# Second block: mixing and experts in one stage by token tiles, and the forget-factor projection in column groups

## The chip, the cores and the metric

The kernel runs on one core of one Trainium2 chip. The metric is the time of one execution on the device, in microseconds (us). A core has a matrix engine (TensorE, PE in the rows, with its weight loads as PEld), a vector engine (VectorE, DVE), an activation engine (ScalarE, ACT), GpSimd (POOL), a queue engine that issues DMAs (SyncE, SP), and 16 DMA engines that all queues share.

## What is computed

Two blocks act on 256 tokens of width 1024, all in float32. The first block has two layers with recurrent (mLSTM), attention and Fourier branches and a feed-forward part; it also carries 256 context tokens in its first layer. The second block mixes (HGRN2 and S5), projects, and then sends each token through 128 retrieved experts. The parts that the change touches, cut from the reference:

```python
# first block, each layer: u = h @ w_in, of which 16 columns are the input and forget gates
i_f, f_f, i_b, f_b = jnp.split(u[4] + gate_b, 4, axis=-1)
...
# second block
mixed = jnp.concatenate([o_hg, o_s5], axis=-1) @ w_out[l]
x = x + gt1 * mixed
h2 = _rmsnorm_2(x, norm_ffn_w[l]) * (1.0 + sc2) + sh2
# experts, h2 in blocks of 128 tokens
qh = (hb @ w_q).reshape(tb, PEER_HEADS, 2, PEER_HALF)          # 8 heads, 2 x 128
s1 = jnp.einsum('thd,nd->thn', qh[:, :, 0], keys1)             # 128 keys each
s2 = jnp.einsum('thd,nd->thn', qh[:, :, 1], keys2)
v1, i1 = lax.top_k(s1, PEER_TOPK)                              # 16 and 16
v2, i2 = lax.top_k(s2, PEER_TOPK)
best, pos = lax.top_k(cand, PEER_TOPK)                         # 16 of the 256 sums
eidx = jnp.take_along_axis(cidx, pos, axis=-1)
gates = jax.nn.softmax(best.astype(jnp.float32), axis=-1).astype(hb.dtype)
act = jax.nn.gelu(jnp.einsum('td,thkd->thk', hb, u_tab[eidx]), approximate=False)
return jnp.einsum('thk,thkd->td', gates * act, v_tab[eidx])
```

## The kernel before

The program is a row of stages. In each stage every engine has its own instruction list, written out by hand, and waits on semaphores; at a stage's end all engines meet (the branch at L303). Nothing reorders the lists: what an engine waits for holds everything behind it.

**First block.** The first stage of a layer projects: `ml_job` multiplies eight 128-row pieces of the normed tokens by 128 columns of weights from a ring of four slots of 1 MB (L794 for 512 tokens across, L803 for 256). After the second job `gate_products` (L819) projects the 16 gate columns. DVE has spread them over 128 columns with zeros between (L1180 memset, L1184 copy), so that TensorE leaves each group of four at rows 0, 32, 64 and 96; ACT reads it there (L1028).

**Second block, mixing stage** (function `mixer`, from L2616). At its end `features` makes the GLU product, DVE and POOL gate the two halves of `merged` (`hg_gated`, `gated`), and TensorE multiplies by `w_out`: `out_tile` (L2805) for eight tiles of 128 columns with all 256 tokens across, each in eight steps. DVE adds each tile to the stream (L2967), ACT squares it (L3039), TensorE sums the squares with a matrix of ones (`out_sum`, L2812), DVE makes mean and reciprocal (L2970, L2971), ACT the root (L3041), DVE scales eight pieces (L2974) and ACT shifts them (L3044). SP meanwhile fetches the query weights of heads 0 to 3 into the ring.

**Second block, expert stage** (function `peer`). SP loads the keys and the query weights of heads 4 to 7 (L3437, L3439). TensorE makes the query of a head for 256 tokens (`query`, L3362), turns the tokens (L3388), and multiplies the query by the keys (`score`, L3380). DVE searches: a unit is one head and one tile of 128 tokens, so there are 16 units, numbered by tile and then by head, of 16 experts each. `halves` takes the best 16 of each half, `numbers` the best 16 of the 256 sums and their indices, `weights` the softmax. Then POOL issues one indirect DMA for each expert slot (L3207): 128 rows of 8 KB, half of it `u_tab`, half `v_tab`. There are 256 such gathers and a ring of eight buffers for them: gather e + 8 waits until TensorE is through with expert e; at the start, gathers 4 to 7 wait for queries 0 to 3, whose weights lie in their buffers. For each expert DVE makes the dot product with the token (L3230), ACT the GELU, the weight and a diagonal matrix (L3319, L3321, L3325), and TensorE adds the diagonal matrix times the `v_tab` half into two banks (L3425). The other steps are placed between the experts by `body`: the search of the unit ahead on DVE, one step of a late head's query after each expert on TensorE, the copies on ACT. After the last expert DVE and ACT do the final norm and SP stores.

## Time and profile before

| | us |
|---|---|
| median of 3 runs | 3245.86 |
| lowest and highest | 3235.61, 3633.01 |
| the profiled execution | 3240.87 |
| its span (first to last instruction) | 3239.0 |
| first indirect gather issued at | 2571.30 |
| last expert's dot product starts at | 3224.01 |
| TensorE busy | 3042.3 (94%) |
| VectorE busy | 1634.6 (50%) |
| ScalarE busy | 806.0 (25%) |
| mean DMA rate | 181 GB/s |

Positions in time are us from the start of the span. The busy shares are means over stages with different limits. The profiled execution took 1.9 us more than its span.

### The profile page before, as it was taken

How to read it: one execution, taken by the hardware profiler on the slowest of the kernel's cores; microseconds unless marked ns; L12 is line 12 of the kernel's file. 1: busy time of each engine (PE TensorE's matmuls, PEld its weight loads, DVE VectorE, ACT ScalarE, POOL GpSimd, SP SyncE). 2: the span in 40 equal slices, each digit the busy share in tenths (PEclk: the TensorE clock that was granted, in tenths of full speed). 3: DMA queues.
4: the chain of work that ended last, by engine and by line, in shares of the span. 5: the costliest groups of instructions: out<-in, count | busy, mean ns of one | idle time of the engine just before them, and what ended most of it. 6: DMA issues, size and time to landing. Idle time of an engine off the chain costs nothing. (4 is left out here: it accounts for less than half of the span.)

```text
span 3239.0 us, 33299 instructions
## 1 busy us (share of the span) xinstructions
PE 3042.3 (94%) x12432; PEld 2117.4 (65%) x12432; DVE 1634.6 (50%) x3601; ACT 806.0 (25%) x1852; POOL 337.4 (10%) x368
## 2 busy tenths in 40 slices
PE   8999999999999999999999999999988899877776
PEld 3566566758888888476776788888877744322222
DVE  3233444367763766313234467452046477777774
ACT  2122244311002100011213420010023244444443
POOL 0000000010000000100000000000000054444442
PEclk9999999999999999999999999999988999999999
DMA  6222111154432544642322234586331599999997
GB/s 236 75 69 63 54 52 53 52 162 130 137 117 65 169 145 132 196 145 80 101 81 65 78 120 151 201 319 223 125 125 55 202 418 420 420 421 421 420 416 306
DMA packets 280767, 584.76 MB, mean 181 GB/s; under 512 B 11736, under 2 KB 231768, under 8 KB 244256
## 3 DMA queue, kind: packets, MB, share of 16 engines
q0 software_dynamic: 51504, 338.98, 26.6%
q1 hardware_dynamic: 229104, 243.66, 23.3%
q8 instruction: 100, 1.64, 0.2%
q14 instruction: 59, 0.48, 0.0%
HBM read 581.52 MB, written 1.08 MB: 180 GB/s over the span
## 5 line engine op out<-in xcount | busy, mean ns | idle before, releaser
L794 PE MATMUL banks<-normed,weight_ring 128*128 128x512 f32 (+1 forms) x1280 | 484.5, 533 | 12.7 <-PEq L307 12.3
L794 PEld LDWEIGHTS banks<-normed,weight_ring 128*128 128x128 f32 x1280 | 243.1, 191 | 232.3 <-issue 221.4
L803 PE MATMUL banks<-weight_ring,normed 128*128 128x256 f32 x1408 | 322.5, 385 | 0.0
L3425 PE MATMUL banks<-weight_ring,work 128*128 128x512 f32 x512 | 249.8, 615 | 59.3 <-ACT work L3325 58.2
L3425 PE MATMUL banks<-work 128*128 128x512 f32 x512 | 252.9, 617 | 54.0 <-ACT work L3325 49.7
L803 PEld LDWEIGHTS banks<-weight_ring,normed 128*128 128x128 f32 x1408 | 266.4, 192 | 54.6 <-issue 19.4
L416 DVE CUSTOM_DVE_ANT_0 work<-work 128x1024 f32<-128x1024 f32 x176 | 209.3, 1223 | 108.2 <-DMA work<-ada_turned 88.5
L2091 PE MATMUL banks<-normed,weight_ring 128*128 128x256 f32 x1088 | 240.3, 384 | 8.7 <-ACT normed L2253 3.8
L2091 PEld LDWEIGHTS banks<-normed,weight_ring 128*128 128x128 f32 x1088 | 209.6, 193 | 38.8 <-ACT normed L2253 4.2
L3425 PEld LDWEIGHTS banks<-weight_ring,work 128*128 128x128 f32 x512 | 89.1, 190 | 199.2 <-ACT work L3325 134.8
L3425 PEld LDWEIGHTS banks<-work 128*128 128x128 f32 x512 | 88.8, 190 | 197.3 <-ACT work L3325 129.6
L1628 PE MATMUL banks<-branches,weight_ring 128*128 128x256 f32 (+1 forms) x656 | 207.5, 478 | 3.4 <-PEq L307 3.4
L3230 DVE CUSTOM_DVE_ANT_0 work<-work,branches 128x1024 f32<-128x1024 f32 x128 | 156.9, 1226 | 97.2 <-DMA work<-experts,branches 96.8
L3230 DVE CUSTOM_DVE_ANT_0 weight_ring<-weight_ring,branches 128x1024 f32<-128x1024 f32 x128 | 156.7, 1225 | 88.8 <-DMA weight_ring<-experts,branches 87.7
L1628 PEld LDWEIGHTS banks<-branches,weight_ring 128*128 128x128 f32 x656 | 124.6, 190 | 84.6 <-issue 75.5
L1652 PE MATMUL banks<-work 128*128 128x256 f32 x744 | 165.6, 379 | 0.0
L3207 POOL DMA_INDIRECT work<-experts,branches x128 | 136.1, 1064 | 242.5 <-PE banks L3425 170.1
L3207 POOL DMA_INDIRECT weight_ring<-experts,branches x128 | 142.0, 1110 | 180.7 <-PE banks L3425 173.1
L2091 PE MATMUL banks<-branches,weight_ring 128*128 128x256 f32 x736 | 159.8, 379 | 0.0
L1652 PEld LDWEIGHTS banks<-work 128*128 128x128 f32 x744 | 141.4, 190 | 19.2
L2091 PEld LDWEIGHTS banks<-branches,weight_ring 128*128 128x128 f32 x736 | 139.8, 190 | 19.0
L3319 ACT ACTIVATE work<-work 128x1 f32<-128x1 f32 x256 | 51.9, 203 | 334.2 <-DVE work L3230 333.9
(495 smaller groups left out, 3930.8 us busy)
## 6 DMA issues: line engine op xcount, KB each, us to landing
weight_ring<-w_in SPq DMA_DIRECT2D x98, 1024.0 KB, 5.2
weight_ring<-w_ffn_in SPq DMA_DIRECT2D x44, 1024.0 KB, 5.2
work<-ada_turned POOLq DMA_DIRECT2D x80, 512.0 KB, 3.8
work<-ada_turned POOLq DMA_DIRECT2D x16, 1536.0 KB, 9.2
weight_ring<-w_ffn_out SPq DMA_DIRECT2D x20, 1024.0 KB, 5.1
weight_ring<-w_out SPq DMA_DIRECT2D x12, 1024.0 KB, 5.2
weight_ring<-w_br_ml SPq DMA_DIRECT2D x8, 1024.0 KB, 5.1
weight_ring<-w_br_da SPq DMA_DIRECT2D x8, 1024.0 KB, 5.2
```

Of the source, the lines that this page charges most:

```text
L416: last = dve.tensor_tensor_reduce(out=out, in0=slot[:, t, :], in1=self.rows[:, row, :], scale=1.0, scalar=0.0, op0=ALU.mult, op1=ALU.add, ...
L794: last = pe.matmul(proj_bank(tile)[:, since:T], w[:, kk, half * P:(half + 1) * P], c.h[:, kk, since:T], start=kk == 0, stop=kk == KT - 1)
L803: last = pe.matmul(proj_bank(tile)[:, x * CHUNK:(x + 1) * CHUNK], c.h[:, kk, j * P:(j + 1) * P], w[:, kk, :], start=kk == 0, stop=kk == KT ...
L1628: ins = pe.matmul(bank(i)[:, cols(p0, p1)], w[:, k - at, half * P:(half + 1) * P], source[:, k, cols(p0, p1)], start=k == 0, stop=k == tot ...
L1652: last = pe.matmul(out[:, half * NCTX:(half + 1) * NCTX], left(k), right(k), start=k == 0, stop=k == KT // 2 - 1)
L2091: ins = pe.matmul(bank(i)[:, 0:NLAT], w[:, k - at, half * P:(half + 1) * P], source[:, k, lat], start=k == 0, stop=k == total - 1)
L3207: pool.indirect_dma_start(out=fetched[e % R], out_offset=None, in_=a["experts"], in_offset=bass.IndirectOffsetOnAxis(ap=experts_u[:, e:e + ...
L3230: dve.tensor_tensor_reduce(out=urows[e % R], in0=urows[e % R], in1=tokens[:, t, :], scale=1.0, scalar=0.0, op0=ALU.mult, op1=ALU.add, accu ...
L3319: act.activation(gl[:, r:r + 1], dot[:, at:at + 1], ACT.Gelu).then_inc(c.act_done, 1)
L3425: last = pe.matmul(c.banks[2 * t + half][:], diag[:, r, :], vrows[r][:, half * 512:(half + 1) * 512], start=e == t * H * K, stop=e == (t + ...
```

## The change

**Second block.** The expert stage becomes part of the mixing stage; `projection_and_experts` gives each engine's list, which `mixer` calls at its end, so no meeting of the engines stands between. The work from the output projection to the scores goes by tiles of 128 tokens: tile 0 is projected, normed and shifted, and head 0's query and score and the first search are made for tile 0 alone. The output projection of token tile 1 stands on TensorE around and behind that; its additions, squares, norm and shifts stand between the experts of units 0 and 1, and its turned tokens in unit 2. Queries and scores of heads 0 to 4 are made for each token tile apart (`PEER_QUERIES`: head, first tile, end), those of heads 5 to 7 for both. The search of unit 1 is no longer started before the first dot product but wholly between the first eight. The loads of `peer_wq` go to eight places outside the ring and are issued earlier, all but head 7's, which waits for the last tile of the output projection. Gathers 4 to 7 wait for the output projection of token tile 1, whose weights are in their buffers. ACT copies the turned tokens instead of DVE.

**First block.** The eight gate products are made in four column groups of 32 columns, two in each, into the rows 0 to 31, 32 to 63, 64 to 95 and 96 to 127 of another bank, after the first job. ACT copies the bank, and one product with the constant `gate_rows` (zeros and ones, a new part of the constants) adds the four and spreads them as before.

```diff
-PEER_EARLY, PEER_LATE, PEER_ROWS_UNIT = (0, 1, 2, 3), (4, 5, 6, 7), 5
+PEER_QUERIES = (*((head, 0, 1) for head in range(5)), *((head, 0, 2) for head in range(5, PEER_H)), *((head, 1, 2) for head in range(5)))
+PEER_AHEAD, PEER_BOTH, PEER_ROWS_UNIT = 3, 5, 5
+PEER_LOADS = ((0,), (1,), (2,), (3, 5, 6, 4), (7,))
...
     wg = scratch[:, 0:KT * 16].rearrange("p (k x) -> p k x", k=KT)
-    wg_apart = scratch[:, KT * 16:KT * 16 + KT * P].rearrange("p (k x) -> p k x", k=KT)
+    wg_apart = scratch[:, KT * 16:KT * 16 + KT * 32].rearrange("p (k x) -> p k x", k=KT)
+    gate_parts = scratch[:, KT * 48:KT * 48 + T]
...
             def gate_products():
+
                 pe.wait_ge(c.gate_apart, 1)
+                for first in range(2):
+                    for strip in range(4):
+                        last = pe.matmul(c.banks[1][32 * strip:32 * strip + 32, :], wg_apart[:, 2 * strip + first, :],
+                                         c.h[:, 2 * strip + first, :], start=first == 0, stop=first == 1)
+                last.then_inc(c.gate_product, 1)
+
+            def gate_total():
+                pe.wait_ge(c.gate_parted, 1)
                 pe.wait_ge(c.constants_loaded, 16)
-                for kk in range(KT):
-                    last = pe.matmul(c.banks[0][:], wg_apart[:, kk, :], c.h[:, kk, :], start=kk == 0, stop=kk == KT - 1)
-                last.then_inc(c.gate_product, 1)
+                pe.matmul(c.banks[0][:], c.constant("gate_rows"), gate_parts, start=True, stop=True).then_inc(c.gate_product, 1)
...
             for number in range(ML_JOBS):
                 ml_job(0, number)
+                if number == 0:
+                    gate_products()
                 if number == 1:
-                    gate_products()
+                    gate_total()
...
                 act.wait_ge(c.gate_product, 1)
+                act.activation(gate_parts, c.banks[1][:], ACT.Copy).then_inc(c.gate_parted, 1)
+                act.wait_ge(c.gate_product, 2)
...
-                apart = wg_apart.rearrange("p k (j x) -> p k j x", j=4)[:, :, :, 0:H]
-                dve.tensor_copy(apart, wg.rearrange("p k (j x) -> p k j x", j=4)).then_inc(c.gate_apart, 1)
+                dve.tensor_copy(wg_apart[:, :, 0:16], wg).then_inc(c.gate_apart, 1)
...
+                if i == SLOTS + 10:
+                    sp.wait_ge(c.pe_out, INPUTS)
+                    sp.wait_ge(c.vec_out, STATES)
+                    rest.early_loads(sp)
                 sp.wait_ge(c.product, FREED[i - SLOTS])
                 sp.dma_start(c.ring[:, i % SLOTS, 0:source.shape[1], :], source).then_inc(c.loaded[i % SLOTS], 16)
-            fetch(c, sp, following, lambda s: sp.wait_ge(c.out_product, 2 * s + 2))
+            rest.sync(sp)
...
+        for e in range(2 * H * K):
+            if e % K == 0:
+                pool.wait_ge(c.ranked, e // K + 1)
+            if e >= R:
+                pool.wait_ge(c.expert_done, e - R + 1)
+            elif e >= R // 2:
+                pool.wait_ge(c.out_product, KT + 2 * (e - R // 2 + 1))
...
+                if u == 0 and at < K // 2:
+                    next(parts[0], None)
+                if u == 0 and at >= K // 2:
+                    added(1, at - K // 2)
+                if u == 1 and at == 4:
+                    inverted(1)
+                if u == 1 and 7 <= at < 7 + KT:
...
+        for tile in range(KT):
+            added(0, tile)
+        inverted(0)
+        for k in range(KT):
+            out_scale(0, k)
+        search = Search(dve, 0)
+        for _ in search.halves():
+            pass
+        assert search.n == IN_HALVES
+        for _ in chain(search.numbers(), search.weights(1)):
+            pass
+        dve.wait_ge(c.token_copied, 2)
+        for u, t in units:
+            body(u, t)
...
+        act.activation(c.work[:, 7184:7185], c.constant("ones")[:, 0:1], ACT.Sqrt)
+        for tile in range(KT):
+            out_square(0, tile)
+        out_root(0)
+        for k in range(KT):
+            out_shift(0, k)
+        copy_query(0)
+        copy_scores(0)
+        copy_tokens(0)
+        exponentials(act, 1)
+        copy_query(1)
+        copy_scores(1)
+        copy_query(2)
+        for u, _ in units:
+            body(u)
...
+        pe.wait_ge(c.merged, 4)
+        pe.wait_ge(c.hg_gated, 2)
+        for tile in range(KT):
+            out_tile(0, tile, 0, 4)
+        pe.wait_ge(c.gated, 4)
+        for tile in range(KT):
+            out_tile(0, tile, 4, 8)
+            if tile >= 2:
+                out_sum(0, tile - 2)
+        pe.wait_ge(c.out_added, 2)
+        out_tile(1, 0, 0, 4)
+        out_sum(0, 6)
+        out_tile(1, 0, 4, 5)
+        out_sum(0, 7)
+        out_tile(1, 0, 5, 8)
+        out_tile(1, 1, 0, 8)
+        query(0)
+        turn_tokens(0)
+        score(0)
+        for tile in range(2, KT):
+            out_tile(1, tile, 0, 8)
+        query(1)
+        query(2)
+        score(1)
+        pe.wait_ge(c.token_copied, 2)
...
+                if PEER_AHEAD + u < len(PEER_QUERIES):
+                    query_product(PEER_AHEAD + u, at // KT, at % KT)
+                if PEER_AHEAD <= PEER_AHEAD + u - 1 < len(PEER_QUERIES) and at == 5:
+                    score(PEER_AHEAD + u - 1)
+                if u == 0 and at == 3:
+                    score(2)
+                if u == 1 and at == 2:
+                    pe.wait_ge(c.score_copied, 3)
+                    for tile in range(KT):
+                        out_sum(1, tile)
+                if u == 2 and at == 4:
+                    turn_tokens(1)
+                if u == PEER_ROWS_UNIT and at % 2 == 0:
+                    turn_rows(at // 2)
...
+    def early_loads(sp):
+        sp.dma_start(keys, a["keys"]).then_inc(c.wq_loaded[0], 16)
+        load(sp, 0)
+        load(sp, 1)
+
+    def sync(sp):
+        sp.wait_ge(c.hg_out, 2)
+        for head in (2, 3, 5, 6):
+            load(sp, head)
+        sp.wait_ge(c.gated, 4)
+        load(sp, 4)
+        sp.wait_ge(c.out_product, 2 * KT)
+        load(sp, 7)
```

How it moves instructions, at three places. In the lists `weight_ring` is the ring, `normed`, `merged`, `stream` and `branches` are large on-chip buffers, and the numbers are the output's rows and columns.

TensorE at the start of a layer of the first block; before:

```order
L794 MATMUL banks<-normed,weight_ring 128x512 x16
L819 MATMUL banks<-normed,merged 128x512 x8
L794 MATMUL banks<-normed,weight_ring 128x512 x32
L803 MATMUL banks<-weight_ring,normed 128x256 x16
L829 MATMUL banks<-constants_sb,work 128x4 x16
```

and now:

```order
L810 MATMUL banks<-normed,weight_ring 128x512 x8
L836 MATMUL banks<-normed,merged 32x512 x8
L810 MATMUL banks<-normed,weight_ring 128x512 x8
L843 MATMUL banks<-merged,constants_sb 128x512
L810 MATMUL banks<-normed,weight_ring 128x512 x32
L819 MATMUL banks<-weight_ring,normed 128x256 x16
```

The eight gate products moved ahead by one job and write 32 rows each; one product of 128 rows stands where they stood.

TensorE from the output projection to the first expert; before (L303 is the meeting of the engines, L3425 the first expert):

```order
L2805 MATMUL banks<-merged,weight_ring 128x256 x8
L2812 MATMUL banks<-normed,constants_sb 128x256 x4
L303 UNCONDITIONAL_BRANCH
L3349 UNCONDITIONAL_BRANCH
L3362 MATMUL banks<-normed,weight_ring 128x256 x16
L3388 MATMUL banks<-constants_sb,normed 128x128 x8
L3380 MATMUL banks<-branches 128x128 x4
L3388 MATMUL banks<-constants_sb,normed 128x128 x8
L3362 MATMUL banks<-normed,weight_ring 128x256 x32
L3380 MATMUL banks<-branches 128x128 x4
L3362 MATMUL banks<-normed,weight_ring 128x256 x16
L3380 MATMUL banks<-branches 128x128 x8
```

and now (L3413 the output projection, L3420 the sums of squares, L3436 queries, L3461 turned tokens, L3453 scores, L3512 experts):

```order
L3413 MATMUL banks<-merged,weight_ring 128x128
L3420 MATMUL banks<-normed,constants_sb 128x128
L3413 MATMUL banks<-merged,weight_ring 128x128 x11
L3436 MATMUL banks<-normed,stream 128x128 x16
L3461 MATMUL banks<-constants_sb,normed 128x128 x8
L3453 MATMUL banks<-branches 128x128 x2
L3413 MATMUL banks<-merged,weight_ring 128x128 x48
L3436 MATMUL banks<-normed,merged 128x128 x16
L3436 MATMUL banks<-normed,work 128x128 x16
L3453 MATMUL banks<-branches 128x128 x2
L3512 MATMUL banks<-work 128x512 x2
```

The meeting is gone, everything is 128 tokens across, and 48 of the output projection's products stand behind the first score.

DVE at the first dot products (L3230 before, L3238 now, where ISA is the dot product); before:

```order
L3173 TENSOR_TENSOR branches<-work 128x16
L3268 COPY branches<-banks 128x512 x2
L3181 TENSOR_REDUCE work<-work 128x1
L3182 RECIPROCAL work<-work 128x1
L3183 TENSOR_TENSOR branches<-work 128x16
L3129 COPY work<-branches 128x256
L3109 MAX work<-work 128x8 x2
L3115 MAX_INDEX work<-work 128x8 x2
L3120 MATCH_REPLACE work<-work 128x128 x2
```

and now, from the same place:

```order
L3175 TENSOR_TENSOR branches<-work 128x16
L3183 TENSOR_REDUCE work<-work 128x1
L3184 RECIPROCAL work<-work 128x1
L3185 TENSOR_TENSOR branches<-work 128x16
L3131 COPY work<-branches 128x256
L3111 MAX work<-work 128x8 x2
L3117 MAX_INDEX work<-work 128x8 x2
L3238 ISA work<-work,branches 128x1024
L3238 ISA work 128x1
L3122 MATCH_REPLACE work<-work 128x128 x2
L3111 MAX work<-work 128x8 x2
L3238 ISA work<-work,branches 128x1024
```

The first dot product stands after two steps of the second search, where before it stood after nearly the whole of its two parts.

## Rows read from the trace of the kernel before

**Rows 1.** Page, the span in 40 slices: busy DMA engines in tenths, and their rate.

```profile
DMA  6222111154432544642322234586331599999997
GB/s 236 75 69 63 54 52 53 52 162 130 137 117 65 169 145 132 196 145 80 101 81 65 78 120 151 201 319 223 125 125 55 202 418 420 420 421 421 420 416 306
```

**Rows 2.** Busy time by stretch: from:to, length, engines (x instructions), granted clock, DMA share, GB/s.

```profile
0.00:2359.00 2359.00, 2305.29 (x9464) 1732.28 (x9464) 1071.20 (x2249) 460.41 (x914) 55.44 (x107) 0.99 0.38 125
...
2538.90:2548.40 9.50, 1.77 (x9) 1.13 (x7) 5.91 (x11) 5.41 (x11) 0.00 (x0) 0.70 0.37 110
...
2584.00:3224.00 640.00, 527.16 (x1210) 209.31 (x1210) 447.21 (x1122) 284.21 (x833) 271.20 (x249) 0.99 1.00 414
3224.00:3239.00 15.00, 3.77 (x8) 1.16 (x7) 5.35 (x8) 3.53 (x7) 0.00 (x0) 0.77 0.08 35
```

**Rows 3.** Timeline, the experts: first and last dot product, and one round of the ring.

```profile
2584.06 1.22 DVE L3230 CUSTOM_DVE_ANT_0 work<-work,branches 128x1024 f32<-128x1024 f32 x1
...
3180.74 1.23 DVE L3230 CUSTOM_DVE_ANT_0 weight_ring<-weight_ring,branches 128x1024 f32<-128x1024 f32 x1 [1.26 <-DMA weight_ring<-experts,branches]
...
3185.28 0.99 POOL L3207 DMA_INDIRECT weight_ring<-experts,branches  x1 [1.55 <-PE banks L3425]
...
3224.01 1.23 DVE L3230 CUSTOM_DVE_ANT_0 weight_ring<-weight_ring,branches 128x1024 f32<-128x1024 f32 x1 [1.26 <-DMA weight_ring<-experts,branches]
```

**Rows 4.** Timeline, from the output projection to the first gather.

```profile
2509.35 14.05 PE L2805 MATMUL banks<-merged,weight_ring 128*128 128x256 f32 x64 [1.55 <-issue]
...
2535.32 3.62 PE L2805 MATMUL banks<-merged,weight_ring 128*128 128x256 f32 x16
...
2541.16 1.75 DVE L2971 RECIPROCAL work<-work 128x256 f32<-128x256 f32 x1
...
2543.92 3.30 ACT L3044 ACTIVATE normed<-normed,modulation 128x256 f32<-128x256 f32 x8 [0.56 <-DVE normed L2974]
...
2548.49 9.35 PE L3362 MATMUL banks<-normed,weight_ring 128*128 128x256 f32 x32 [7.82 <-PEq L307]
...
2558.55 1.14 PE L3380 MATMUL banks<-branches 128*128 128x128 f32 x8
...
2560.36 0.29 DVE L3129 COPY work<-branches 128x256 f32<-128x256 f32 x1 [0.75 <-ACT branches L3295]
...
2571.30 1.01 POOL L3207 DMA_INDIRECT work<-experts,branches  x1 [63.06 <-DVEq L3174]
```

**Rows 5.** Groups with shapes apart: count, then busy us, mean ns.

```profile
L1308 DVE SCALAR_TENSOR_TENSOR branches<-banks,vectors_sb,work 128x128 f32<-128x128 f32 x48 | 14.4, 343 | 22.2 <-PE banks L868 22.2
L2967 DVE SCALAR_TENSOR_TENSOR stream<-banks,modulation,stream 128x256 f32<-128x256 f32 x8 | 3.9, 484 | 26.3 <-PE banks L2805 26.3
L3325 ACT ACTIVATE work<-constants_sb,work 128x128 f32<-128x128 f32 x256 | 102.7, 401 | 8.5
```

**Rows 6.** Timeline, TensorE: two scores in a row.

```profile
2582.02 2.01 PE L3380 MATMUL banks<-branches 128*128 128x128 f32 x16
```

**Rows 7.** DMA issues in 2540 to 2571: KB each, us to landing.

```profile
merged<-peer_wq SPq DMA_DIRECT2D x2, 1024.0 KB, 11.9
normed<-peer_wq SPq DMA_DIRECT2D x1, 1024.0 KB, 5.8
```

**Rows 8.** The gathers L3207 issued from 2571 to 2600.

```profile
DMA to landing us min/median/max: 8.1/8.9/12.4
```

**Rows 9.** Timeline, start of the first layer.

```profile
46.73 0.23 DVE L1184 COPY merged<-merged 128x128 f32<-128x128 f32 x1 [6.88 <-DMA merged<-w_in]
...
55.22 7.03 PE L819 MATMUL banks<-normed,merged 128*128 128x512 f32 x16
...
62.08 23.34 PE L794 MATMUL banks<-normed,weight_ring 128*128 128x512 f32 x54
```

**Rows 10.** Timeline, TensorE: 64 records with 32 weight columns, in four column groups.

```profile
2375.96 0.59 PE L2651 MATMUL banks<-normed,weight_ring 128*128 128x256 f32 x2
2376.48 1.96 PE L2662 MATMUL banks<-branches,work 128*32 128x128 f32 x64
```

**Rows 11.** Timeline, ACT: table loads around a unit's exponentials.

```profile
2790.07 1.28 ACT L3189 ACT_TABLE_LOAD   x1
...
2792.08 1.28 ACT L3319 ACT_TABLE_LOAD   x1
```

571 lines of the change are left out of this document (280 added, 291 removed).

## The prediction

> **What bounds the kernel now.** I read the slices first: from the 33rd on the DMA engines stand at nine tenths and move about 420 GB/s, and nowhere before [rows 1]. So the kernel has two regimes. In the first 2359 us TensorE is busy for 2305 [rows 2]: time taken from TensorE there shortens the run one for one. From 2584 to 3224 TensorE is busy for 527 of 640 us, DVE for 447, ACT for 284, and the DMA share is 1.00 [rows 2]. That is the stage of the 256 gathers, 1 MB each. Its length is fixed by bytes: from the first gather's issue at 2571.30 [rows 4] to the last dot product at 3224.01 [rows 3] it is 652.7 us. The dot products run from 2584.06 to 3224.01, 2.51 us each, and the late ones wait for DMA [rows 3]. Nothing on DVE, ACT or TensorE in this stage is worth anything while the ring keeps the DMA engines fed. What counts is when the first gather is issued. Between the output projection's start at 2509.35 and that issue lie 62.0 us of serial work: projection, norm, query, score, search [rows 4]. The last 15.0 us hold the end of the last expert, the final norm and the store [rows 2], and the change leaves them.
>
> **The second block, up to the first gather.** I cost the path piece by piece.
>
> Projection: 64 products are two records each. With 256 tokens across, 64 records take 14.05 us, 0.220 each, and the last ends at 2535.32 + 3.62 = 2538.94 [rows 4]. With 128 tokens half of that is 0.110; sixteen records of 128 by 128 took 2.01 us, 0.126 each [rows 6]. I take 0.118. Token tile 0 needs 128 records, and six of the sums (12 records) come before its last product: 140 x 0.118 = 16.5 us, so it ends at 2525.9, 13.0 us earlier. The other token tile's projection costs as much again. Sixteen to 24 of its records fill the norm, where TensorE now idles (1.77 us busy of 9.5 [rows 2]); 96 stand behind the first score, 11.3 us, under the search of 10.9 us. They end within half a microsecond of it, and only gather 7 and head 7's load wait for their end.
>
> Norm: the last product to the last shift is 2538.94 to 2543.92 + 3.30 = 2547.22, 8.3 us [rows 4]. All pieces become half as wide. DVE's addition shows what that brings: 343 ns for 128 by 128 against 484 for 128 by 256 [rows 5]; ACT gets nearer to its floor, 401 ns at 128 wide [rows 5]; the reciprocal of 1.75 us [rows 4] is the one that should halve. 8.3 x 343/484 = 5.9 us, between 4.2 (half) and 8.3 (no gain). Gain 2.4.
>
> The meeting of the engines, 2547.22 to 2548.49 [rows 4], goes: 1.3 us.
>
> Query: it took 9.35 us [rows 4]. Now its first half follows the shifts piece by piece, and only 16 records and a tail stand behind the last shift, 2.2 us. Gain 7.2; if the first half is not hidden, 5.3.
>
> Turned tokens, score and copies: 2548.49 + 9.35 = 2557.84 to 2560.36 is 2.5 us [rows 4]; half the score and half the copy save some 0.5 (0 to 1). ACT takes over the token copies while DVE searches.
>
> The search, 2560.36 to 2571.30, 10.9 us [rows 4], is the same.
>
> Sum: 13.0 + 2.4 + 1.3 + 7.2 + 0.5 = 24.4 us, so the first gather is issued at about 2546.9. With every term at its worse end it is 18, at its better end 27.
>
> **What the gathers meet there.** In the trace the last loads of `peer_wq` are issued at the expert stage's start, 23 us before the first gather, and land within 12 [rows 7]. Now the load of head 7 is issued when the output projection is done, at about the first gather, and shares the DMA engines with it. Loads of 1024 KB landed after 5.8 us for the first and 11.9 at the median of the third and fourth [rows 7], 2.4 us for each place in the row; I take 3.0 us (0 if it gets through first, 5.8 if it is served wholly ahead). The other seven are issued before the output projection or at its start and have 37 us. Net gain of this part: 21.4 us.
>
> Behind the first gather the ring must not run dry. A late round shows the price of a lap: the dot product starts at 3180.74, and the gather that its expert frees is issued at 3185.28, 4.5 us later [rows 3]; a gather lands at the least 8.1 us after its issue [rows 8]. That makes 12.6 us, and the next use of a buffer is due after eight gathers, 20.1 us. So a dot product may be 7.5 us behind its data before the DMA engines see it. Now unit 0's first eight dot products carry a whole search: 8 x 1.3 (1.23 [rows 3] and a short read-out) + 11.3 = 21.7 us against 20.1, a lag of 2. The next eight carry eight additions (2.7 us) and the first part of the following search (about 3.4): 16.6 us, and they catch up. In unit 1, DVE's step before the fifth dot product waits for the sums that TensorE makes after the third expert, and makes mean and reciprocal; ACT then takes the root between two dot products, and that costs two table loads of 1.28 on top of the two that each unit has [rows 11]. I add 2 + 1.3 + 2.6 = 6 us of lag at once, gone by the unit's end. It fits under 7.5, with little over. I cost it at nothing; the cover is the ring's queue. Without it, each us of lag beyond 7.5 is a us at the end, once.
>
> **The first block.** The eight gate products take 62.08 - 55.22 = 6.86 us, 0.429 a record [rows 9], on TensorE, which has no idle time around them. What column groups cost is in another stage: 64 records of 128 columns in four groups took 1.96 us, with a gap of about 0.1 us at the change of shape [rows 10], which is four times as fast as one after another. Sixteen records of 512 columns are as many columns: 1.96 us. The new product is two records of 0.429, 0.86 us. Gain 6.86 - 1.96 - 0.86 = 4.0 in each of two layers, 8.1 us. ACT's copy has the next job, 6.9 us, to hide under. The gate weights are ready at 46.96 [rows 9]; the second job is sixteen records of 0.429 before 55.22, so the first ends at about 48.3, and the products, moved ahead of the second, still find them ready, with 1.4 us to spare. Bounds: 0 if the loads or ACT take the time back, 9.4 if the groups have no gap at all.
>
> Here a rule speaks against the change. The Trainium skill, TensorE: Matmul & The Clock Gate, section "Packing small matmuls — row/col tiling", lists 2.38 times for three column tiles, so 0.79 of full effect; by that the sixteen records would take 2.2 us and the gain be 3.8 a layer. Rows 10 show four times in this kernel, and I stay with them; the difference is half a microsecond.
>
> **Sum.** 24.4 - 3.0 + 8.1 = 29.5 us off the profiled execution's 3240.87: **3211 us**. That execution lies between the runs of 3235.61 and 3245.86, the second of which is the median shown; against the median it would be 1.1% less. A measurement of this kernel can tell about 2%, 65 us, from no change, and no term comes near that.
>
> **The rivals.**
>
> A, the halves are not half. If TensorE's weight loads, 128 columns each whatever the tokens, set the pace, a record of 128 by 128 could cost as much as one of 256, 0.220. From the output projection's start to the first score there are 140 + 22 + 16 + 4 records: 182 x 0.10 = 18 us later, gain 11 in all, 3229 us. Against it: the score's 16 records, each with its own weights, at 0.126 [rows 6]. The full form has 0.03.
> The same page of the Trainium skill, section "Back-to-back issue gap", gives 81 ns for pairs of load and product at 128 columns where the product alone takes 56, 1.45 times. As a mechanism here: a record of 0.110 becomes 0.160, 182 x 0.042 = 8 us later than my sum, 3219 us. Chance 0.05; rows 6 speak against it.
>
> B, the ring runs dry in units 0 and 1. The lag is priced above at 6 of 7.5 us; were it 12 the end comes 4.5 later, and with a late first dot product 8 later: 3215 to 3219 us. For it: DVE has 21.7 us of work against 20.1 just then. Against: it is DVE at 447 of 640 later. Chance 0.12.
>
> C, the first block keeps its time, because another engine takes over at the gates: 3219 us. Against: TensorE at 2305 of 2359. Chance 0.04.
>
> D, **slower than before**: scores arrive just in time for each unit. Before, they were a unit ahead; now for units 2 to 12 the step before DVE's ninth dot product needs the score that TensorE makes after that unit's or the previous unit's sixth expert and ACT copies before its ninth. If DVE stalls there by L us, it loses L - 7.5 each time, eleven times. It decides from L = 7.5; to pass 3241 L must be above 10.2. For it: the hand-over chain passes three engines inside one unit. Against: from the sixth expert's product to the ninth dot product there are about 3 us, so I expect a stall near 1. Chance 0.02.
>
> E, the change does not do what it says: the first gather waits for something else, such as the load of the keys or of head 0 behind the mixing's loads, and stays near 2571: 3233 us. These loads are issued some 90 us ahead. Chance 0.02.
>
> The forecast with its own terms, 3204 to 3218, has 0.72.
>
> **Range and chances.** Worst ends of the forecast: 18 - 5.8 + 4 = 16 off, 3225; best: 27 + 9.4 = 36 off, 3205. The two ordinary runs lie 5 us to either side of the profiled one, and I add that below and 3 above: 3200 to 3228. B, C and the mild form of A lie in it. Faster by over 2% needs more than twice the sum, 0.02. Slower by over 2% needs D with a stall of 16 us or an odd median, 0.02. Within 2%: 0.96.
>
> **What would show it.** First gather at 2571 - 24 - 8 = 2539 in the new span, with no meeting of the engines before it; the new 128 by 128 projection records 0.12 apart; gate products of about 2 us; 652 to 656 us from first gather to last dot product, the DMA share at 1.00 throughout. A distance over 660 us is B or D, and a dip of the DMA rate in units 0 and 1 tells them apart. A first gather near 2555 is A. The prediction is wrong if the stage of the gathers is not a matter of bytes, so that its order or the lag of its first rounds changes its pace.

## The result, and the profile after

The changed kernel takes 3211.97 us (median of 4 runs, 3207.51 to 3214.9), against 3243.73 for the kernel before (4 runs, 3235.61 to 3633.01). The run of 3633.01 us was in a second, slower state of the chip and is left out of the ratio, so the kernel before counts with 3241.60. The ratio is 0.9909, with an interval of 0.9895 to 0.9923. The forecast was 3211 us, in the range of 3200 to 3228. The profiled execution took 3213.26 us with a span of 3211.3, 27.6 less than the profiled execution before.

The page of the kernel after, the span in 40 slices, busy DMA engines in tenths and GB/s:

```profile
DMA  6212111144341544642322234577432699999997
GB/s 238 86 59 66 53 53 53 53 164 131 120 137 53 170 145 135 196 148 80 105 79 79 63 115 148 198 273 277 137 112 95 245 420 420 381 417 420 420 421 322
```

Against [rows 1] two things differ. The stage of the gathers starts earlier (245 GB/s in the 32nd slice, where 202 stood). And the 35th slice has 381 GB/s where 420 stood: the DMA engines went short of work, which I had not foreseen.

The timeline from the output projection to the first gather, after; it answers to [rows 4]. L3413 is the projection, L3420 the sums, L3286 the reciprocal, L3291 and L3347 scale and shift, L3436 queries, L3461 the tokens' turn, L3453 the score:

```profile
2501.61 10.06 PE L3413 MATMUL banks<-merged,weight_ring 128*128 128x128 f32 x88 [1.55 <-issue]
...
2518.65 0.39 PE L3420 MATMUL banks<-normed,constants_sb 128*128 128x128 f32 x2
...
2519.40 0.95 DVE L3286 RECIPROCAL branches<-branches 128x128 f32<-128x128 f32 x1
...
2521.12 2.45 ACT L3347 ACTIVATE normed<-normed,modulation 128x128 f32<-128x128 f32 x8 [0.42 <-DVE normed L3291]
...
2521.66 4.23 PE L3436 MATMUL banks<-normed,stream 128*128 128x128 f32 x32 [0.17 <-ACT normed L3347]
...
2526.60 0.61 PE L3453 MATMUL banks<-branches 128*128 128x128 f32 x4
...
2527.67 0.29 DVE L3131 COPY work<-branches 128x256 f32<-128x256 f32 x1 [4.75 <-ACT branches L3323]
...
2537.97 0.37 SPq L3535 DMA_DIRECT2D merged<-peer_wq  x1
2538.61 1.01 POOL L3206 DMA_INDIRECT work<-experts,branches  x1 [38.12 <-DVEq L3176]
```

From the projection's start to the first gather's issue it is now 37.00 us; before it was 61.95. The gather is issued at 2538.61, where the prediction had 2539. A projection record costs 10.06 / 88 = 0.114 us. The query ends at 2525.89, 2.3 us behind the last shift (2521.12 + 2.45), because its first half runs while ACT still shifts. Search 0 starts at 2527.67 and takes 10.94 us, as before. There is no meeting of the engines between. The load of head 7 goes out 0.64 us ahead of the first gather.

The start of both layers of the first block, TensorE, after; it answers to [rows 9]. L836 are the eight gate products in column groups, L843 the new product:

```profile
48.66 1.92 PE L836 MATMUL banks<-normed,merged 128*32 128x512 f32 x16
50.51 7.13 PE L810 MATMUL banks<-normed,weight_ring 128*128 128x512 f32 x16
57.48 1.02 PE L843 MATMUL banks<-merged,constants_sb 128*128 128x512 f32 x2
58.34 27.63 PE L810 MATMUL banks<-normed,weight_ring 128*128 128x512 f32 x64
...
1464.85 1.92 PE L836 MATMUL banks<-normed,merged 128*32 128x512 f32 x16
1466.71 7.13 PE L810 MATMUL banks<-normed,weight_ring 128*128 128x512 f32 x16
1473.68 1.02 PE L843 MATMUL banks<-merged,constants_sb 128*128 128x512 f32 x2
1474.54 13.98 PE L810 MATMUL banks<-normed,weight_ring 128*128 128x256 f32 x64
```

From start to start the gates hold TensorE for (50.51 - 48.66) + (58.34 - 57.48) = 2.71 us in the first layer and 1.86 + 0.86 = 2.72 in the second. The same job took 6.86 us in each before. That is 8.3 us off.

The last dot product after, on DVE; it answers to the last of [rows 3]:

```profile
3196.28 1.23 DVE L3238 CUSTOM_DVE_ANT_0 weight_ring<-weight_ring,branches 128x1024 f32<-128x1024 f32 x1 [1.25 <-DMA weight_ring<-experts,branches]
```

From the first gather's issue it is 657.67 us; before, 652.71. I had expected 655.7, and named 652 to 656 as the sign. So the stage of the gathers has become 5.0 us longer, and the 15.0 us behind it are as before. In sum, between the two profiles: 7.7 (the projection starts at 2501.61 in place of 2509.35), plus 24.95, minus 4.96, is 27.7 us.

**Where the stage grew.** The timeline around the 88th dot product, in unit 5, after. L3475 turns the final norm's rows on TensorE, L3335 copies them on ACT, L3512 is an expert, L3206 a gather, L3323 the copy of a score, L3131 DVE's first step of a search:

```profile
2766.43 1.23 DVE L3238 CUSTOM_DVE_ANT_0 weight_ring<-weight_ring,branches 128x1024 f32<-128x1024 f32 x1 [1.23 <-DMA weight_ring<-experts,branches]
...
2767.45 0.60 PE L3475 MATMUL banks<-constants_sb,stream 128*128 128x128 f32 x4
...
2768.09 0.60 ACT L3335 ACTIVATE branches<-banks 128x512 f32<-128x512 f32 x1 [2.73 <-PE banks L3475]
2769.59 1.98 PE L3512 MATMUL banks<-weight_ring,work 128*128 128x512 f32 x4 [1.54 <-ACT work L3381]
...
2774.47 0.60 PE L3475 MATMUL banks<-constants_sb,stream 128*128 128x128 f32 x4
2774.68 0.94 POOL L3206 DMA_INDIRECT weight_ring<-experts,branches  x1 [1.90 <-PE banks L3512]
2775.10 0.60 ACT L3335 ACTIVATE branches<-banks 128x512 f32<-128x512 f32 x1 [4.71 <-PE banks L3475]
2776.46 0.58 ACT L3323 ACTIVATE branches<-banks 128x512 f32<-128x512 f32 x1
...
2777.07 0.29 DVE L3131 COPY work<-branches 128x256 f32<-128x256 f32 x1 [9.41 <-ACT branches L3323]
2777.92 1.23 DVE L3238 CUSTOM_DVE_ANT_0 work<-work,branches 128x1024 f32<-128x1024 f32 x1
```

TensorE turns rows behind the expert at an even place of unit 5, and ACT copies them ahead of its work for the very next expert. So ACT waits for TensorE (2.73, then 4.71 us), and TensorE then waits for ACT (1.54). The two take turns where they used to overlap. DVE goes on until it needs the next score (L3323), which stands behind those copies in ACT's list, and there it stops for 9.41 us. The two dot products start 11.5 us apart. In the kernel before, the copy stood two experts behind the turn (`2 <= at < 10`, `copy_rows(at - 2)`, against `at < 8`, `turn_rows(at)`), and no two dot products are over 3.5 us apart there.

Busy time by stretch (columns as in [rows 2]), after, the 50 us behind that stall:

```profile
2780.00:2830.00 50.00, 43.64 (x144) 22.82 (x145) 37.40 (x99) 22.72 (x72) 21.44 (x20) 1.00 0.94 357
```

At 420 GB/s less 357, over 50 us, the DMA engines lack 7.5 us of work. GB/s here are a mean over all 16 engines.

### The profile page after: what moved, and what is told of

Read it like the earlier page. It is cut to its first block and busy times, and to the rows that moved or that the text cites. A ratio compares the mean times of both kernels' runs of the same rounds, so it can differ in the third digit from the quotient of the medians.

```text
span 3211.3 us, 33966 instructions
## 1 busy us (share of the span) xinstructions
PE 3023.5 (94%) x12740; PEld 2129.7 (66%) x12740; DVE 1633.9 (51%) x3615; ACT 813.7 (25%) x1888; POOL 337.5 (11%) x368
## 5 line engine op out<-in xcount | busy, mean ns | idle before, releaser
L810 PE MATMUL banks<-normed,weight_ring 128*128 128x512 f32 (+1 forms) x1280 | 485.3, 534 | 12.8 <-PEq L322 12.4
L3512 PE MATMUL banks<-work 128*128 128x512 f32 x512 | 252.7, 617 | 52.6 <-ACT work L3381 51.9
L3512 PE MATMUL banks<-weight_ring,work 128*128 128x512 f32 x512 | 248.8, 610 | 55.0 <-ACT work L3381 54.2
L2117 PE MATMUL banks<-normed,weight_ring 128*128 128x256 f32 x1088 | 241.3, 385 | 10.6 <-DMA weight_ring<-w_ffn_in 3.9
L3512 PEld LDWEIGHTS banks<-work 128*128 128x128 f32 x512 | 88.4, 191 | 165.8 <-ACT work L3381 93.7
L3238 DVE CUSTOM_DVE_ANT_0 weight_ring<-weight_ring,branches 128x1024 f32<-128x1024 f32 x128 | 156.8, 1225 | 79.7 <-DMA weight_ring<-experts,branches 76.8
L3512 PEld LDWEIGHTS banks<-weight_ring,work 128*128 128x128 f32 x512 | 87.7, 189 | 165.3 <-ACT work L3381 102.7
L3238 DVE CUSTOM_DVE_ANT_0 work<-work,branches 128x1024 f32<-128x1024 f32 x128 | 156.8, 1225 | 71.9 <-DMA work<-experts,branches 67.3
L3206 POOL DMA_INDIRECT weight_ring<-experts,branches x128 | 141.9, 1108 | 182.1 <-PE banks L3512 179.4
L3206 POOL DMA_INDIRECT work<-experts,branches x128 | 136.4, 1066 | 220.9 <-PE banks L3512 176.5
L402 POOL DMA_DIRECT2D work<-ada_turned x96 | 50.9, 530 | 768.0 <-DVEq L437 768.0
```

What stands on the lines that cost most here:

```text
L402: pool.dma_start(self.slots[n % ADA_SLOTS][:, 0:nt, :], self.a["ada_turned"][which, :, t0:t0 + nt, :]).then_inc(c.ada_loaded[n % ADA_SLOTS ...
L810: last = pe.matmul(proj_bank(tile)[:, since:T], w[:, kk, half * P:(half + 1) * P], c.h[:, kk, since:T], start=kk == 0, stop=kk == KT - 1)
L2117: ins = pe.matmul(bank(i)[:, 0:NLAT], w[:, k - at, half * P:(half + 1) * P], source[:, k, lat], start=k == 0, stop=k == total - 1)
L3206: pool.indirect_dma_start(out=fetched[e % R], out_offset=None, in_=a["experts"], in_offset=bass.IndirectOffsetOnAxis(ap=experts_u[:, e:e + ...
L3238: dve.tensor_tensor_reduce(out=urows[e % R], in0=urows[e % R], in1=tokens[:, t, :], scale=1.0, scalar=0.0, op0=ALU.mult, op1=ALU.add, accu ...
L3512: last = pe.matmul(c.banks[2 * t + half][:], diag[:, r, :], vrows[r][:, half * 512:(half + 1) * 512], start=e == t * H * K, stop=e == (t + ...
```

## The experiments

Two measures run through them. The median times are good to 5 to 9 us, by their intervals. The distance from the first gather's issue to the last dot product, taken from each profile, is much steadier: 657.67 and 657.89 in two executions of the changed kernel, 654.46 and 654.07 in two of `rows_later`, 652.71 before and 652.82 with the first block's part alone.

### Each part alone

`gates_only` is the kernel before with the first block's part: column groups, the new product, and the constant matrix that it needs.

```diff
-                for kk in range(KT):
-                    last = pe.matmul(c.banks[0][:], wg_apart[:, kk, :], c.h[:, kk, :], start=kk == 0, stop=kk == KT - 1)
...
+                for first in range(2):
+                    for strip in range(4):
+                        last = pe.matmul(c.banks[1][32 * strip:32 * strip + 32, :], wg_apart[:, 2 * strip + first, :],
...
+                pe.matmul(c.banks[0][:], c.constant("gate_rows"), gate_parts, start=True, stop=True).then_inc(c.gate_product, 1)
```

> The kernel before with the change of the first block alone: gate products in four column groups after the first job, ACT's copy, one product with gate_rows. Theory: 2 x (6.86 - 1.96 - 0.86) = 8.1 us less on TensorE, all of it at the end, so 8 us less than before, ratio 0.9975, with 16 records of L819 in 2 us where they took 7. In the changed kernel the output projection started 7.7 us earlier. Rival C: the time does not move (ratio 1.000), because another engine or the loads take it back.

Measured: 3233.58 us (12 runs) against 3240.72 (17 runs), ratio 0.9986, interval 0.9972 to 1.0. That is 4.5 us off, 0 to 9.1; the medians themselves are 7.1 apart. The 8.3 us read from the rows lie inside the interval, near its end, but a gain of nothing lies inside it too. Two further readings help. The spread of the times goes with the granted TensorE clock, the mean over an execution as a share of the full one: of the 17 runs of the kernel before, the fastest, 3230.84 us, had 0.987 and the slowest, 3247.6 us, 0.981 (the correlation over the 17 is -0.93), and 0.001 less clock goes with some 2.2 us more. `gates_only` had 0.001 less clock on average; taken at the same clock, an estimate from these 29 runs, it is 7.2 us faster, give or take 1.6. And the output projection starts at 2509.35 and 2514.86 in the two profiles with the old gates, but at 2496.34 to 2508.30 in the ten with the new ones. So the gain of the first block is there, though its size is known no better than that.

`stage_only` is the changed kernel with the gates as they were (the same lines the other way round).

> The changed kernel with the first block as before. Theory: the output projection starts at 2509 as before, the first gather 37 us later (62 before), first gather to last dot product 657 us as in the changed kernel (652.7 before): 20 us less than before, ratio 0.9938, and with gates_only the two add up to the whole, 28 us. Rival: the two edits are not independent and the sum misses the whole by over 4 us.

Measured: 3219.16 us (6 runs), ratio 0.9936, interval 0.9919 to 0.9953: 21 us off. The first gather is issued 37.00 us behind the projection's start (2514.86 to 2551.86), as in the whole, and the last dot product starts 658.07 us later. By the rows that is 24.95 - 5.36 = 19.6 us. The product of the two ratios is 0.9922 and the whole change has 0.9909, which is 4.2 us apart: just over the 4 us of the rival, but inside the intervals, so the times decide nothing here. By the rows, 8.3 + 19.6 = 27.9 us against 27.7 for the whole, the parts add up.

### The whole projection ahead of the query

```diff
         out_tile(1, 0, 5, 8)
-        out_tile(1, 1, 0, 8)
+        for tile in range(1, KT):
...
+            out_tile(1, tile, 0, 8)
         query(0)
         turn_tokens(0)
         score(0)
-        for tile in range(2, KT):
-            out_tile(1, tile, 0, 8)
```

> The changed kernel with the output projection of token tile 1 wholly before the first query instead of behind the first score (96 records of 128 by 128 moved ahead, tile 4 waiting for the mean's read of its bank). Theory: up to the first gather the path is serial, so the first gather comes later by 96 x 0.113 = 10.9 us, less about 1 us in which TensorE waits for the norm, and the end with it: 10 us more than the changed kernel, ratio to before 0.994. Rival: the head start is not worth its length, because the ring's fill or the second search sets the end: under 5 us more.

TensorE in `projection_first`, and the first gather:

```profile
2499.60 10.06 PE L3413 MATMUL banks<-merged,weight_ring 128*128 128x128 f32 x88 [1.55 <-issue]
...
2516.87 13.34 PE L3413 MATMUL banks<-merged,weight_ring 128*128 128x128 f32 x118
2530.04 3.74 PE L3436 MATMUL banks<-normed,stream 128*128 128x128 f32 x32
```

The second token tile's products run in one row of 118 records at 0.113, and the query begins at 2530.04, 30.4 us behind the projection's start in place of 20.1. The first gather is issued at 2546.50, 46.9 us behind that start, 9.9 later than in the whole. Measured: 3218.76 us (4 runs), ratio 0.9935, interval 0.9913 to 0.9956: some 8 us slower than the whole by the ratios (0.9935 against 0.9909), whose intervals overlap. The trace is the firmer evidence: the gather comes 9.9 us later, and the distance from there to the last dot product is 0.8 us shorter (656.84 against 657.67). Hiding the second tile's projection under the search is worth about what its 96 records cost, 10.9 us, less 1.

### The rows of the final norm copied later

```diff
-                if u == PEER_ROWS_UNIT and at % 2 == 1:
-                    copy_rows(at // 2)
+                if (u == PEER_ROWS_UNIT and at % 2 == 0 and at >= 2) or (u == PEER_ROWS_UNIT + 1 and at == 0):
+                    copy_rows((K * (u - PEER_ROWS_UNIT) + at) // 2 - 1)
```

> The changed kernel, but in unit 5 ACT copies the turned row blocks before the experts 2, 4, 6 ... (one expert later than now, the last before expert 0 of unit 6). In the trace of the changed kernel unit 5 shows gathers issued every 3.8 to 4.2 us, a stall of 11.5 us before a dot product, and a DMA rate of some 300 to 360 GB/s for 50 us. Theory: before every odd expert ACT waits for a turn that TensorE makes behind the even expert, so the two engines take turns, some 7 us for two experts against 5.0 of data; the lag passes the ring's cover and costs about 8 us at the end. With the copy one expert later that is gone: first gather to last dot product 649 to 652 us instead of 657.7, and 6 to 8 us less than the changed kernel, ratio to before about 0.9885. Rival: the dip in unit 5 is a hiccup of the DMA engines, and nothing changes (0.9909).

Busy time by stretch in `rows_later`, the same 50 us:

```profile
2780.00:2830.00 50.00, 45.18 (x143) 23.22 (x142) 35.90 (x91) 22.64 (x68) 22.74 (x22) 1.00 1.01 420
```

The dip is gone, the 88th dot product comes 5.3 us behind the 87th, and from the first gather's issue to the last dot product it is 654.46 us, 3.2 less. The cause of the dip is shown. Its price was not foreseen: I had expected 649 to 652 us. How far the dip reaches is best seen at the gathers. The 104th is issued 266.39 us behind the first in the changed kernel and 253.63 us behind it here, so the turn-taking held the gathers up by as much as 12.8 us. Measured: 3211.13 us (5 runs), ratio 0.9909, interval 0.989 to 0.9928, no difference from the whole that a median can tell.

Since 7.5 us of missing transfers had cost only 3.2, I ran both again, on one chip.

> The whole change, unedited, beside rows_later_again on the same chip. By the distances from first gather to last dot product it should be 3.2 us slower than that (657.7 against 654.5 us). The other theory, that the stall while rows are turned back costs nothing at the end, has no difference. The second question is when the first dot product starts: 13.6 us after the first gather was issued in four executions, 9.0 in two with the same order of work; if it goes by execution and not by kernel, either can show here, and the distance stays at 657 to 658.

> rows_later, unedited, beside whole_again: 3.2 us faster than it if the stall counts, 654 to 655 us from first gather to last dot product whichever of the two starts the first dot product shows.

Measured: 3212.82 us for the whole (6 runs, ratio 0.9915, 0.9896 to 0.9934) and 3213.42 for `rows_later_again` (6 runs, 0.9908, 0.9888 to 0.9928). The distances are 657.89 and 654.07 us. So the stall costs 3.2 to 3.8 us in the stage, and the medians can't show it: what comes ahead of the stage varies more. The same kernel started its projection at 2501.61 in one profile and at 2496.59 in the other.

### How far a dot product may lag

`rows_later` with useless writes on DVE ahead of the fifth dot product of units 9, 11 and 13, each waiting for the last. `delay_9` has 5 at each place, `delay_16` 9, `delay_5` 2:

```diff
+                if u in (9, 11, 13) and at == 4:
+                    for step in range(5):
+                        count = 3 + (9, 11, 13).index(u) * 5 + step
+                        dve.memset(mixed, 0.0).then_inc(c.averaged, 1)
+                        dve.wait_ge(c.averaged, count)
```

> The kernel with the rows turned back later (rows_later, 3211.13 us; 654.5 us from first gather to last dot product), and on DVE five writes of 128 by 1024 zeros, one after another, ahead of the fifth dot product of units 9, 11 and 13: about 8.8 us of lag each time. They add work that the result does not use. The question is how much lag the ring covers. Theory 1, the prediction's: 7.5 us of cover, so each delay costs 1.3 us, 4 in all: 658 to 659 us from first gather to last dot product, time 3215. Theory 2, the landing is set by one DMA engine that is behind the others, whose queue is the fuller: cover of about 11 us, nothing is lost, 654.5 us and 3211, while the overall rate may dip. Theory 3, no cover: 3 x 8.8, 3237.

> As delay_9, with nine writes, 15.8 us of lag, at each of the three places. Theory 1, cover 7.5 us: 8.3 us lost each time, 25 in all: 679 us from first gather to last dot product, time 3236. Theory 2, cover 11 us: 4.8 lost each time, 14 in all: 669 us and 3225. Theory 3, no cover: 47, 3258. In both of the first, the gaps between dot products behind the delay are short until the data runs out, and then wait for DMA.

DVE in `delay_16`, the first delay:

```profile
2925.79 1.23 DVE L3243 CUSTOM_DVE_ANT_0 work<-work,branches 128x1024 f32<-128x1024 f32 x1 [0.42 <-DMA work<-experts,branches]
...
2929.25 1.76 DVE L3236 MEMSET merged<- 128x2048 f32 x1 [0.49 <-DVE work L3172]
2931.51 1.76 DVE L3236 MEMSET merged<- 128x2048 f32 x1 [0.49 <-DVE merged L3236]
...
2949.12 1.22 DVE L3243 CUSTOM_DVE_ANT_0 weight_ring<-weight_ring,branches 128x1024 f32<-128x1024 f32 x1
2950.90 1.23 DVE L3243 CUSTOM_DVE_ANT_0 weight_ring<-weight_ring,branches 128x1024 f32<-128x1024 f32 x1 [0.25 <-DVE branches L3175]
```

A write takes 1.76 us, but the next one starts 2.26 behind it, and the profile puts the 0.49 between them down to the wait for the one before; the expectations had left the 0.49 out. So the lag was larger than they say: the dot products are 23.3 us apart in `delay_16` and 14.3 in `delay_9`, against 2.5 undisturbed, a lag of 20.8 and of 11.8 us. (The writes are 128 by 2048, as the rows show, and not 128 by 1024 as the expectations say.)

`delay_9`: 3223.58 us (10 runs), ratio 0.996, interval 0.9942 to 0.9978; 669.78 us from first gather to last dot product. Against 654.46 that is 15.3, or 5.1 for each delay. `delay_16`: 3253.8 us (10 runs), ratio 1.0043, interval 1.0024 to 1.0061; 697.65 us, 43.2 more, 14.4 each. The cover is then 11.8 - 5.1 = 6.7 us by the one and 20.8 - 14.4 = 6.4 by the other. Behind it every us counts: 9.0 us more lag cost 9.3. The theory of a cover of 11 us falls: by it `delay_9` would have lost some 2 us in all. The prediction's 7.5 was 1 us too much.

> As delay_9, with two writes, 5.0 us of lag (2 x 2.26 and 0.5), at each of the three places. delay_9 held dot products up by 11.8 us and lost 5.1 each time, delay_16 by 20.8 and lost 14.4: a cover of 6.5 us. If the cover is a threshold, 5.0 us cost nothing: 654.5 us from first gather to last dot product, as in rows_later, time as rows_later. The rival, that each delay costs a share of itself (0.43 and 0.69 of it above): some 0.3 x 5.0 x 3 = 4.5 us, 659 us.

`delay_5`: 3218.47 us (4 runs), ratio 0.9929, interval 0.9901 to 0.9957; two dot products are 7.5 us apart at each delay, 5.0 of lag, and the distance is 654.69 us, 0.2 more than in `rows_later`. So three delays below the threshold cost nothing. The median is 5 to 7 us above those of `rows_later`; the profile puts that ahead of the stage, with the projection's start at 2508.30.

This also helps with the 7.5 us of missing transfers that cost only 3.2. Busy time by stretch in `rows_later`, the last 14 us before its last dot product (3194.15):

```profile
3180.00:3184.00 4.00, 2.99 (x8) 0.86 (x6) 1.68 (x4) 1.80 (x6) 0.00 (x0) 1.00 1.01 420
3184.00:3188.00 4.00, 3.49 (x8) 1.34 (x8) 2.46 (x4) 0.96 (x4) 0.00 (x0) 1.00 0.40 164
3188.00:3192.00 4.00, 3.00 (x8) 0.99 (x7) 1.57 (x3) 1.74 (x6) 0.00 (x0) 1.00 0.06 25
```

and in `delay_5`, the same stretches before its own (3200.00):

```profile
3186.00:3190.00 4.00, 2.99 (x7) 0.85 (x7) 1.55 (x4) 1.80 (x6) 0.00 (x0) 1.00 1.01 420
3190.00:3194.00 4.00, 3.50 (x8) 1.20 (x8) 2.46 (x4) 1.09 (x4) 0.00 (x0) 1.00 1.01 420
3194.00:3198.00 4.00, 2.99 (x7) 1.13 (x7) 1.72 (x3) 1.60 (x6) 0.00 (x0) 1.00 0.76 315
```

In `rows_later` nearly all transfers are over some 8 us before the last dot product, and from 3188 on the DMA share is 0.06, about one engine of 16 (the trace doesn't name it). The dot product waits all that time, so it waits for the last engine's part, and the others have run ahead of that one. In `delay_5` they have lost about 5 us of this lead, and the end is where it was.

The changed kernel lies between. The last 14 us before the last dot product, first in `rows_later`, then after:

```profile
3180.15:3194.15 14.00, 10.97 (x23) 3.61 (x23) 6.47 (x13) 5.39 (x18) 0.00 (x0) 1.00 0.42 173
```

```profile
3182.28:3196.28 14.00, 10.97 (x23) 3.61 (x23) 6.48 (x13) 5.39 (x18) 0.00 (x0) 1.00 0.66 272
```

A share of 0.66 in place of 0.42 over 14 us is 3.4 us of lead that the others no longer have. With the 3.2 to 3.8 us that the end comes later, this makes 6.6 to 7.2, about the work that was missing. So a dip of the mean rate is no measure of lost time: it is paid partly out of this lead and partly in time, and time was paid although some lead was left. What the end goes by is the lag against the cover.

### Without head 7's load

```diff
-                slot(big[:, 2 * D:4 * D]), slot(spent), mixed]
+                slot(big[:, 2 * D:4 * D]), slot(spent), slot(spent)]
...
-        load(sp, 7)
```

> rows_later without the load of head 7's query weights; head 7 uses head 6's, so its scores are not the reference's. One load of 1024 KB that shares the DMA engines with the first gather is gone. Theory 1, the prediction's term: 3.0 us back, 651.5 us from first gather to last dot product, time 3208; the first data of the first gather move 1.7 us after its issue in place of 3.6. Theory 2, the load is hidden: 654.5 us and 3211, although the first data come earlier.

Measured: 3210.39 us (5 runs), ratio 0.9913, interval 0.9886 to 0.994; 654.09 us from first gather to last dot product, as with the load. Its first data move 1.7 us after the issue in place of 3.6, and yet nothing is gained. The first 40 us of transfers in `no_head_7`:

```profile
2545.30:2585.30 40.00, 29.53 (x115) 17.42 (x114) 28.17 (x88) 16.40 (x47) 17.95 (x17) 0.87 1.00 400
```

and in `rows_later_again`:

```profile
2546.70:2586.70 40.00, 34.22 (x116) 18.71 (x115) 33.95 (x100) 18.77 (x55) 20.55 (x18) 0.91 1.02 420
```

A rate of 400 against 420 over 40 us is 1.9 us: in this execution the DMA engines did run short in unit 0. What stands out there is ACT's copy of score 1, with which the search of unit 1 begins. Two steps of that search stand ahead of the first dot product in DVE's list, as the list of the change shows (its text says that they stand wholly between the first eight). In `no_head_7`:

```profile
2549.87 0.61 PE L3453 MATMUL banks<-branches 128*128 128x128 f32 x4
...
2555.14 0.38 ACT L3323 ACTIVATE branches<-banks 128x256 f32<-128x256 f32 x1 [8.25 <-remote]
```

and in `whole_again`:

```profile
2539.90 0.61 PE L3453 MATMUL banks<-branches 128*128 128x128 f32 x4
...
2540.55 0.38 ACT L3323 ACTIVATE branches<-banks 128x256 f32<-128x256 f32 x1 [3.64 <-PE banks L3453]
```

In the second the copy starts 0.04 us after the score's end, in the first 4.66 after it, and the trace names nothing in the core that released it. The first dot product then starts 13.6 us after the first gather's issue in place of 9.0. It is the late form in four profiles (the changed kernel, `delay_9`, `delay_16`, `no_head_7`) and the early one in six (`whole_again`, the two of `rows_later`, `delay_5`, `stage_only`, and `projection_first`, where the copy follows the score at once), and the changed kernel shows both, so the order of work doesn't set it. The chip might: the three late ones of which the chip is recorded ran on chip 1, and the six early ones on chips 2 and 14. No kernel was profiled on chip 1 and on another with its chip recorded, so this stays open.

The form by itself costs nothing at the end (657.67 us late, 657.89 early, both with the load). I take it that the load makes everything land 1.9 us later, which is cover enough, and that without it the late form uses up what the load had cost; but a run without the load in the early form is missing, and the kernel before has 408 GB/s in the first 40 us of its transfers and still the shortest distance. So this run leaves the theory that the load is hidden standing. Two others bound the price: `rows_later`, which has the load and no dip, is 1.4 to 1.8 us above the kernel before, and `projection_first`, where the load is through before the gathers, is 0.8 to 1.2 below the whole and `stage_only` (656.84 against 657.67 to 658.07). Other things differ in both pairs. The load costs between nothing and 2 us.

## Why the prediction was right, and where not

The forecast was 29.5 us off, from one profiled execution to another, and those two show 27.7. Against the 3241.60 that the ratio goes by, the median is 29.6 off. That this is so near is luck: the interval of the ratio alone is 4.5 us to either side. What carries the forecast is that the parts came out one by one.

**The projection and the norm** were 13.0 + 2.4. The last shift ended 37.87 us behind the projection's start in [rows 4], and now 21.96: 15.9. A record is 0.114 us where I took 0.118.

**The meeting and the query** were 1.3 + 7.2. The query ended 10.6 us behind the last shift, and now 2.3: 8.3.

**Turn, score and copies** were 0.5. They took 2.52 us and now take 1.78: 0.7. The search is the same. In sum 24.95 against 24.4.

**Rival A**, that 128 tokens cost nearly as much as 256, falls by 0.114 against 0.220. The Trainium skill, TensorE: Matmul & The Clock Gate, section "Back-to-back issue gap", gives 81 ns for pairs of load and product at 128 columns, against 56 for the product alone, 1.45 times; this trace has 0.114 against half of 0.220, 1.04 times.

**The first block** was 8.1 and measures 8.3. Sixteen records in four column groups take 1.85 us, 0.116 each, against 0.429 one after another, 3.7 times with the changes of shape. Rival C, that another engine takes it back, is not excluded by the medians (4.5 us, 0 to 9.1). The estimate at equal clock, 7.2 us, and the start of the projection in twelve profiles speak against it.

**Head 7's load** was 3.0 and costs 0 to 2. The first data of the gathers do come later, 3.6 us behind the issue in place of 1.7, so 1.9 is what the load takes there; the 3.0 was read from a queue in which more loads stood. That the 1.9 reaches the end isn't shown by any run.

**The ring in units 0 and 1** was costed at nothing, and that held in the changed kernel: its first 40 us of transfers have 420 GB/s. But the forecast was nearer the edge than it knew. The cover is 6.5 us and not 7.5, the first dot product can be 4.6 us late, and in the run with a late first dot product and no load ahead the DMA engines did run short by 1.9 us. That is rival B's mechanism, and the distance did not grow by it (654.09 us).

**Rival D**, scores just in time, has the stall I gave it, about 1 us: before the ninth dot product the distance is 3.4 to 3.6 us in place of 2.5 in most units, with no dip; in unit 1, with the sums on top, it is 5.5. The exceptions are unit 5 and, in its wake, unit 6 (4.9 to 6.6). What DVE waited for in unit 5 was the copy of a score, as in rival D, with a stall of 9.0 us, over the 7.5 from which the rival decides; but what held the copy was the turn-taking, which the rival doesn't have.

**What failed** is the sentence "the DMA share at 1.00 throughout", and behind it the list of what is moved past what. I followed DVE's list through units 0 and 1 and ACT's only through its table loads. I did not see that ACT's copies of the final norm's rows went from two experts behind the turn to the very next one, although the code of both kernels says so. The stage took 5.0 us more where 3.0 were costed, and 3.2 to 3.8 of the 5.0 are this. The size doesn't follow from the cover: the dot product was 9.0 us late and the gathers up to 12.8, which less 6.5 would be 2.5 and 6.3. It stood in the place of a load that is cheaper than costed, so the total looked better than its parts. The prediction named as its sign of being wrong that the order in this stage changes its pace; by these 3.2 to 3.8 us it does.

## What to carry to other kernels

When a stage is bound by transfers with a ring before it, write down the ring's cover (here 6.5 us; one lap less issue and landing gave 7.5) and then check every place where an engine waits for a step that another engine made only just before, above all copies that stand ahead of the chain's own work in an in-order list: a single lag counts only beyond the cover, and then one for one (5.0, 11.8 and 20.8 us here). Let a copy stand two rounds behind what it copies. Where effects are smaller than the spread of the medians, compare a distance inside the trace between two events of the stage; here it repeats within 0.4 us while the time moves by 10.

## What the runs showed that I had not expected

- The mean DMA rate may fall short by some 5 us of work without any cost at the end (`delay_5`): all engines but about one run ahead of the last at the stage's end (share 0.06 in the last 6 us). Yet the changed kernel lost 3.2 to 3.8 us while part of that lead was left.
- A copy on ACT starts 4.6 us late in four of the ten profiles of the new stage, always at the same place and by the same amount, with no releaser inside the core. What holds it stays open, and whether it goes by the chip too. The instruction fetches on the DMA queues look alike in both forms, one packet about 1 us ahead of the first gather, and don't tell them apart.
- Writes in a row that wait for each other come 2.26 us apart for 1.76 of work: the profile puts 0.49 us down to the wait of an engine for itself. No run has the same writes without the waits.
- The run-to-run spread of the kernel before goes with the granted clock: 3230.84 us at 0.987, 3247.6 at 0.981. The correlation over 17 runs is -0.93, so this is most of what blurs the medians.
